# First modulation summed by VectorE, silu when the vectors are there, latent keys ahead of the values

## The reference

```python
cond = silu(c)                                    # 1024 values
for i in range(4):
    mod = cond @ ada_w[i] + ada_b[i]              # 1024 x 6144
    sh_a, sc_a, g_a, sh_f, sc_f, g_f = split(mod, 6)
    h = rms_norm(x, norm_g[i, 0]) * (1 + sc_a) + sh_a
    y = mixer(h)                                  # MLA in layers 0 and 3
    ...

def mla_mixer(h):                                 # 8 heads
    q_lat, kv_lat, k_pe = split(h @ w_in, [256, 384])
    q = rms_norm(q_lat, q_norm) @ w_q_up          # 128 + 64 (rope) a head
    kv = rms_norm(kv_lat, kv_norm) @ w_kv_up      # 128 keys, 128 values a head
    # q, k get rope parts; causal softmax in query blocks of 128; then @ w_out
```

## Time and profile before

| | us |
|---|---|
| median of three runs | 4621.73 |
| lowest and highest | 4619.29, 4622.21 |
| the profiled execution | 4615.57 |
| its span, first to last instruction | 4613.8 |
| TensorE busy | 4290.5 (93%) |
| mean granted TensorE clock | 0.947 |

### The profile page before, as it was taken

One profiled execution on the slowest core, in us unless ns is written; L12 is line 12 of the kernel. 1 busy time (PEld: TensorE's weight loads), 2 busy tenths in 40 slices (PEclk: granted clock), 3 DMA queues, 4 the chain that ended last, 5 costly groups with the idle time before them and its releaser, 6 DMA issues.

```text
span 4613.8 us, 66591 instructions
## 1 busy us (share of the span) xinstructions
PE 4290.5 (93%) x24442; PEld 2275.2 (49%) x24442; DVE 2171.8 (47%) x4420; ACT 2498.2 (54%) x3432; POOL 1951.3 (42%) x1077
## 2 busy tenths in 40 slices
PE   7989989889989988998989989998899899999999
PEld 5544444444444434444544443445455565556555
DVE  4654220644152423424521021426469887586684
ACT  4557444667444535744567444356456555655544
POOL 1134333444333324443034333220135456858767
PEclk9989989989989998998989989798899899999999
DMA  4346222046222223622022222220123456958768
GB/s 160 144 166 237 96 80 83 16 171 223 96 84 79 73 69 143 254 96 82 24 73 100 100 89 86 71 71 1 37 98 132 164 196 216 336 194 290 261 216 300
DMA packets 160504, 623.63 MB, mean 135 GB/s; under 512 B 17824, under 2 KB 17952, under 8 KB 156816
## 3 DMA queue, kind: packets, MB, share of 16 engines
q1 hardware_dynamic: 123120, 483.65, 30.0%
q0 software_dynamic: 37152, 136.80, 8.0%
HBM read 618.29 MB, written 2.10 MB: 134 GB/s over the span
## 4 chain that ended last, share of the span: by engine, by line
PE 58%; issue 17%; POOL 12%; DVE 9%; DMA 2%; ACT 2%; POOLq 0%; DVEq 0%; ACTq 0%
PE ps L779 15%; PE ps L780 15%; PE ps L781 15%; POOL halves L592 8%; POOL rows L660 3%; PE ps L830 2%; DMA rows<-v_rows,h 1%; DVE rows L2593 1%; PE ps L1373 1%; PE ps L786 1%; PE ps L788 1%; PE ps L787 1%; PE ps L717 1%; POOL x L642 1%; DVE rows L2592 1%
## 5 line engine op out<-in xcount | busy, mean ns | idle before, releaser
L592 POOL TENSOR_TENSOR halves<-ring,halves 128x1024 f16<-128x1024 f32 x718 | 1583.1, 2206 | 2438.9 <-ACT halves L1480 2205.0
L779 PE MATMUL ps<-h,halves 128*128 128x512 f16 (+1 forms) x2912 | 1061.3, 364 | 42.7 <-DVE h L2162 21.1
L780 PE MATMUL ps<-h,halves 128*128 128x512 f16 (+1 forms) x2912 | 1060.6, 364 | 0.0
L781 PE MATMUL ps<-h,halves 128*128 128x512 f16 (+1 forms) x2912 | 1059.4, 364 | 0.0
L1477 ACT ACTIVATE ring<-ring 128x1024 f32<-128x1024 f32 x718 | 754.7, 1051 | 479.7 <-DMA ring<-wstream 406.5
L779 PE MATMUL ps<-rows,halves 128*128 128x512 f16 (+2 forms) x2544 | 914.5, 359 | 83.7 <-POOL halves L592 40.1
L780 PE MATMUL ps<-rows,halves 128*128 128x512 f16 (+2 forms) x2544 | 913.0, 359 | 0.0
L781 PE MATMUL ps<-rows,halves 128*128 128x512 f16 (+2 forms) x2544 | 912.1, 359 | 0.0
L1480 ACT ACTIVATE halves<-ring 128x1024 f16<-128x1024 f32 x718 | 758.8, 1057 | 22.8
L779 PEld LDWEIGHTS ps<-h,halves 128*128 128x128 f16 x2912 | 287.0, 99 | 354.2 <-issue 60.8
L781 PEld LDWEIGHTS ps<-h,halves 128*128 128x128 f16 x2912 | 287.3, 99 | 296.6 <-issue 13.1
(11 more groups left out here) (290 smaller groups left out, 5053.5 us busy)
## 6 DMA issues: line engine op xcount, KB each, us to landing
ring<-wstream SPq DMA_DIRECT2D x718, 512.0 KB, 3.3
rows<-ada SPq DMA_DIRECT2D x96, 768.0 KB, 5.1
rows<-ada_first SPq DMA_DIRECT2D x24, 1024.0 KB, 5.5
x<-x_in POOLq DMA_DIRECT2D x1, 2048.0 KB, 13.3
rows<-u_rows,h POOLq DMA_INDIRECT x128, 5.8
rows<-v_rows,h POOLq DMA_INDIRECT x128, 6.2
out<-x SPq DMA_DIRECT2D x8, 256.0 KB, 2.7
rows<-phase_nsa SPq DMA_DIRECT2D x1, 1600.0 KB, 6.6
```

Of the source, the lines that this page charges most:

```text
L592: nc.gpsimd.tensor_tensor(halves[:, j % RING, 1, :], ring[:, j % RING, :], halves[:, j % RING, 0, :], ALU.subtract).then_inc(s_wlow, 1)
L779: nc.tensor.matmul(out_, high, act16[:, 0, :], start=first, stop=False)
L780: nc.tensor.matmul(out_, high, act16[:, 1, :], start=False, stop=False)
L781: return nc.tensor.matmul(out_, low, act16[:, 0, :], start=False, stop=last)
```

## The change

- `EARLY_SUMS` is 8: VectorE sums all eight chunks of the first modulation, three of them, then its two pair sums of squares, three more, the inverse roots, then the last two. TensorE only sums the finished buffer over the partitions, with `ada_sums(0, 16, 8)`, after the token norms are spread.
- The vectors have a semaphore of their own, `s_vec`. ScalarE and VectorE start silu and the chunk sums when the vectors are there, and wait for `x` and the matrices (`s_const` at 32) only before the squares and before the modulation.
- The slots for keys and values change places. TensorE makes the key tiles first, through the four banks as before; then the value tiles, through banks 4 to 7, with a wait that the inverses have been copied from bank 5 (`s_latcopied`) and with their own count of reads. ScalarE reads value tiles only after all key tiles have been read. VectorE starts the key products when the query and rotation tiles have been read.
- `row_blocks` on TensorE gets `late`: scores start when all but the last `late` = 8 reads (the value tiles) are done, and the wait for all of them stands before the first transpose.

```diff
-EARLY_SUMS = 4
+EARLY_SUMS = C
 ADA_PIECES = 6
...
         s_const = sem("consts_loaded")
+        s_vec = sem("vectors_loaded")
         s_phase = sem("phase_loaded")
...
         s_keys = sem("key_tiles")
+        s_latcopied = sem("latent_inverses_copied")
         s_negmax = sem("row_max_normed")
...
-            pool.dma_start(vec[:, :], vecs).then_inc(s_const, 16)
+            pool.dma_start(vec[:, :], vecs).then_inc(s_vec, 16)
             pool.dma_start(x[:, :, :], x_in).then_inc(s_const, 16)
...
-            def row_blocks(rows, places):
-
-                pe.wait_ge(s_evac, seen["tile"])
+            def row_blocks(rows, places, late):
+                pe.wait_ge(s_evac, seen["tile"] - late)
                 base_seg, base_pt, base_group, base_row = seen["seg"], seen["pt"], seen["group"], seen["row"]
...
+                        if i == lag:
+                            pe.wait_ge(s_evac, seen["tile"])
                         pe.wait_ge(s_normed, base_row + i - lag + 1)
...
                 input_means(h, IN_NORM[0])
-                seen["ada"] += EARLY_SUMS
-                pe.wait_ge(s_adas, EARLY_SUMS)
-                b = bank()
-                for j in range(2 * C):
-                    nc.tensor.matmul(b[:, j:j + 1], ada_sum[:, j * P:j * P + P], ones[:, 0:1], start=(j == 0), stop=False,
-                                     skip_group_check=True)
                 token_norms(IN_NORM[1])
-                pe.wait_ge(s_cond, 1)
-                for k in range(EARLY_SUMS, C):
-                    pe.wait_ge(s_adae[k], 16)
-                    for j in range(2 * C):
-                        mm = nc.tensor.matmul(b[:, j:j + 1], ada_early[:, k, j * P:j * P + P], cond[:, k:k + 1],
-                                              start=False, stop=(k == C - 1), skip_group_check=True)
-                mm.then_inc(s_tile, 1)
+                ada_sums(0, 2 * C, EARLY_SUMS)
...
                 w = slot()
-                for tb in range(TB):
-                    for half in range(2):
-                        b = bank()
-                        mm = split_tokens(b, w, slice(half * T, half * T + T), latent16[:, 2],
-                                          slice(tb * P, tb * P + P), True, True)
-                        mm.then_inc(s_used if tb == TB - 1 and half else s_tile, 1)
-                w = slot()
                 for m in range(8):
...
+                w = slot()
+                pe.wait_ge(s_latcopied, layer // 3 + 1)
+                for tb in range(TB):
+                    for half in range(2):
+                        t = seen["tile"]
+                        if 2 * tb + half >= 4:
+                            pe.wait_ge(s_evac, t - 3)
+                        seen["tile"] += 1
+                        mm = split_tokens(ps[:, 4 + (2 * tb + half) % 4, :], w, slice(half * T, half * T + T),
+                                          latent16[:, 2], slice(tb * P, tb * P + P), True, True)
+                        mm.then_inc(s_used if tb == TB - 1 and half else s_tile, 1)
                 wait(s_rot, "rot", 5)
-                row_blocks(mla_rows(), mla_places)
+                row_blocks(mla_rows(), mla_places, 8)
...
                       "nsa": lambda l: nsa()}
-            pe.wait_ge(s_const, 48)
+            pe.wait_ge(s_vec, 16)
+            pe.wait_ge(s_const, 32)
             pe.wait_ge(s_ones, 4)
...
                             copy(y[:, 4 + i, :])
-                act.wait_ge(s_latinv, seen["lat"])
-                for m in range(8):
-                    b = tile(int(m == 7))
-                    nc.scalar.activation(arena[:, 20 + m, :], b, ACT.Identity, scale=kv_inv[:, m // 2:m // 2 + 1])\
-                        .then_inc(s_evac, 1)
...
                 use(1)
+                act.wait_ge(s_latinv, seen["lat"])
+                act.wait_ge(s_evac, seen["tile"])
+                for m in range(8):
+                    if m < 7:
+                        seen["tl"] += 1
+                        act.wait_ge(s_tile, seen["tl"])
+                    else:
+                        seen["used"] += 1
+                        act.wait_ge(s_used, seen["used"])
+                    seen["tile"] += 1
+                    nc.scalar.activation(arena[:, 20 + m, :], ps[:, 4 + m % 4, :], ACT.Identity,
+                                         scale=kv_inv[:, m // 2:m // 2 + 1]).then_inc(s_evac, 1)
+                feed(seen["used"] + AHEAD)
                 row_blocks(mla_rows(), mla_places)
...
-            act.wait_ge(s_const, 48)
             act.wait_ge(s_ones, 3)
+            act.wait_ge(s_vec, 16)
             nc.scalar.activation(cond[:, :], v("c", 0, C), ACT.Silu).then_inc(s_cond, 1)
             nc.scalar.preload_act_table_set("sqrt_and_others")
+            act.wait_ge(s_const, 32)
             for k in range(C):
...
                 dve.wait_ge(s_latspread, seen["mla"] + 1)
-                link(nc.vector.tensor_copy(rinv, ps[:, KV_NORM[1], :]))
+                nc.vector.tensor_copy(rinv, ps[:, KV_NORM[1], :]).then_inc(s_latcopied, 1)
+                dve.wait_ge(s_latcopied, seen["mla"] + 1)
                 for m in range(8):
...
                     else:
-                        dve.wait_ge(s_used, seen["used"] + 4 + 3 + 1 + 1)
+                        dve.wait_ge(s_used, seen["used"] + 4 + 3 + 1)
                     if m == 0:
-                        tiles(6 + 8)
+                        tiles(6)
                     mul(arena[:, 12 + m, :], ps[:, (seen["tile"] + m) % LIN_BANKS, :], rinv)\
                         .then_inc(s_evac, 1)
-                tiles(8)
+                seen["tile"] += 16
                 row_blocks(mla_rows(), mla_places,
...
-            dve.wait_ge(s_const, 48)
+            dve.wait_ge(s_vec, 16)
             if stages[0][1] < LAYERS:
                 dve.wait_ge(s_cond, 1)
-                ada_third(0, range(EARLY_SUMS // 2))
+                ada_third(0, range(3))
                 square_pairs(h)
-                ada_third(0, range(EARLY_SUMS // 2, EARLY_SUMS))
+                ada_third(0, range(3, 6))
                 inverse_roots()
+                ada_third(0, range(6, C))
+                dve.wait_ge(s_const, 32)
                 tiles(1)
...
                 feature_slots(np.concatenate([q[:, :, MLA_NOPE:].reshape(256, -1), q[:, :, :MLA_NOPE].reshape(256, -1)], 1)),
-                kv[:, :, 1].reshape(1, P, SLOT), kv[:, :, 0].reshape(1, P, SLOT),
+                kv[:, :, 0].reshape(1, P, SLOT), kv[:, :, 1].reshape(1, P, SLOT),
                 feature_slots(a["mla_w_out"][j])]
...
```

## The result

| | us |
|---|---|
| before, median of 4 runs | 4621.81 |
| after, median of 4 runs | 4574.24 (4568.31 to 4575.36) |
| ratio after to before, with its 95% interval | 0.9896 (0.9878 to 0.9913) |
| profiled execution and span, after | 4568.31, 4566.3 |
| mean granted TensorE clock | 0.954 (before 0.947) |

What follows compares the result with a forecast made beforehand. TensorE, busy for 93% of the span, was taken to bound the kernel. Minus 20.1 us (start) and minus 6.3 us (latent stages) make minus 26.4, from a 4621.73 us median to 4595 us, range 4586 to 4603.

Steps and rivals of the forecast that it cites:

- Part 1: First modulation at the start: 128 single-column matmul records go, column matmuls end at 45.4 us, minus 20.1 us.
- The turns with GpSimd: Start: two GpSimd subtractions and VectorE's last two chunk sums exclude each other, ending the sums at 38.3, not 34.8 us.
- rival A: Start: VectorE isn't held up by GpSimd, so the first modulation gives 23.6 us; 4591.8 us, chance 17%.
- Part 2: Latent stage of both MLA layers: keys ahead of values start the scores 3.15 us earlier, twice, minus 6.3 us.
- ScalarE's lateness: Latent stage: ScalarE gains only 1.5 us, but the first row is ready 1.0 us before its transpose at 136.1.
- Rival C: Latent stage: the new order gives nothing, the wait only moves to the first transposes; 4601.6 us, chance 13%.
- The sum: Whole kernel: minus 20.1 minus 6.3 = minus 26.4 us, so 4595 us; forecast's chance 50%.
- rival B: Layer 3's first score rows: without idles the half-clock fall may stay away, 7.9 us more; 4587.4 us, chance 17%.
- So the whole kernel moves by this amount: Everything behind the first projection: nothing has a clock of its own, so all shifts by the start's 20.1 us.
- Rival D: Start: the eighth chunk becomes the pacemaker and the kernel is slower if it lands from 62.3 us on; chance 1%.

Runs made afterwards that it cites:

- e7: Changed kernel, but GpSimd makes its first two weight subtractions only after VectorE's eight chunk sums; ratio 0.9888 to the kernel before.
- e14: Kernel before with only the first latent-stage idle filled by unread matmuls, the 1.51 us ahead of the scores kept; 4629.27 us, ratio 0.9999.
- second part alone: Kernel before with only keys ahead of values and values in other banks, the start as before; 4605.16 us, ratio 0.9942.
- e1: Kernel before with only the first modulation's part of the change, the latent stage as before; 4611.85 against 4631.45 us, ratio 0.9963.
- e10: Kernel before, not edited, run once more with a second profile; 4633.17 us in one run.
- e13: Kernel before with only the idle ahead of the scores filled by unread matmuls, the first idle kept; 4615.24 against 4629.49 us, ratio 0.9973.
- e9: Changed kernel, not edited, run again with a second profile; 4583.63 against 4627.96 us for the kernel before, ratio 0.9905.
- e3: Changed kernel with four of the sixteen column matmuls on the finished modulation sum made twice; ratio 0.9905 to the kernel before.
- e12: Changed kernel with GpSimd's subtractions held behind the sums and unread matmuls in TensorE's waits at the start; 4579.73 us, ratio 0.9900 to the kernel before.

## Why the prediction was wrong

- **Part 1, the start: right.** 45.4 was forecast for the end of the column matmuls, 45.46 came; VectorE's last sum at 38.3, came at 38.42; the projection at 48.7, came at 48.88. The turns with GpSimd, the one real choice in this part, were right (e7), and rival A is out. Two small readings were off and cost nothing: the squares started at 18.00, not 17.3, and silu ran at 10.03, not 8, since its table load waited for the vectors, until 8.74; in the kernel before that load was over before any input had landed (below). Alone the part measured 17 us (11 to 24).
- **Part 2, the order: right.** 10.7 us from keys to scores, both idles gone (with an unchanged start, 59.81 us from the first projection to the first score in e14, with the old order and its first idle filled, and 56.68 with the second part alone), ScalarE's lateness hidden with 0.9 us to spare, 1.0 forecast. Rival C is out: the first row was ready at 111.30, its transpose started at 112.21.
- **The sum: wrong, in the term that it left out.** The prediction said of the half clock in layer 3, "layer 0 had the same idles and no fall, so it isn't the idles alone", gave rival B 17%, and put its price at 7.9 us in one layer. The runs showed it to be the idle ahead of the scores, in both layers as a rule: with that idle, layer 3 fell in four profiles of four (before, e1, e10, e14) and layer 0 in three of four; without it, or with 1.23 us, in none of the twelve others. In the table below, a fall cost some 8 us in layer 3, and 7.9 (e1) or 12.6 us (e10, e14) in layer 0. What both are worth in the medians is 12.5 us (e13; 8 to 17), taken by a line that moves nothing. 26.4 + 12.5 = 38.9, where 47.6 and 44 us were measured (interval of the second 37 to 51).
- **The step behind that.** One absent event in layer 0 is one sample, and I used it as evidence against a mechanism that layer 3 showed at its full price. "The median shown is 6.2 above it, with the same work" passed over a hint that single executions differ. It was no more than a hint: the changed kernel's two profiled executions are 5.9 and 6.7 us under their medians as well, with no fall behind the latent stage, so the distance doesn't say which stretch is missing.
- **A second step that failed: "So the whole kernel moves by this amount".** It doesn't move as one piece. These are the parts of the span, in us, with the row blocks taken up to the next matmul on converted weights (207.48 in the kernel before):

| profile | to first projection | to layer 0's first score | its row blocks | to layer 3's first score | its row blocks | to the end |
|---|---|---|---|---|---|---|
| before | 68.81 | 63.72 | 74.95 | 2017.66 | 82.92 | 2305.70 |
| before again (e10) | 69.17 | 62.40 | 87.57 | 2017.31 | 82.92 | 2312.00 |
| second idle kept (e14) | 69.54 | 59.81 | 87.58 | 2017.34 | 82.91 | 2312.97 |
| first idle kept (e13) | 69.60 | 59.72 | 74.98 | 2019.87 | 75.04 | 2311.41 |
| first part alone (e1) | 48.75 | 59.82 | 82.85 | 2022.77 | 82.92 | 2311.57 |
| changed | 48.88 | 56.72 | 74.87 | 2010.36 | 74.94 | 2300.57 |
| changed again (e9) | 48.80 | 56.79 | 74.87 | 2010.43 | 74.93 | 2309.06 |
| delayed by the smaller amount (e3) | 50.22 | 58.99 | 74.88 | 2016.10 | 74.94 | 2308.65 |

From the first profile of the kernel before to that of the changed kernel, the columns differ by 19.9, 7.0, 0.1, 7.3, 8.0 and 5.1 us. The forecast's terms are 20.1, 3.15 in the second and 3.15 in the fourth. The second column has 3.4 us more from a half-clock stretch ahead of layer 0's latent stage, with TensorE busy in all of it, which the changed kernel's two profiles lack:

```profile
94.20:101.00 6.80, 6.80 (x18) 0.50 0.12 47
```

The fourth has some 4 us more from the work between the layers, where the same number of matmul records kept TensorE busy for 1873.0 us in place of 1879.9; in e3 they took 1881.1. So in these two profiles layer 3's fall is 8.0 of the missing 21 us. Most of the rest is the 3.4 and 4 us, which were largely back when the start moved by 1.3 us (e3: 58.99 and 2016.10), and 5.1 us behind layer 3.

- **Open.** 5 to 9 us between 38.9 and the measured medians. The table shows places where a single profile gains that much, and shows them for the changed kernel twice, alike to 0.1 us up to layer 3. But its other runs took 5.6 to 7.1 us longer, in the first set at a mean granted clock of 0.951 against the profile's 0.954, and no profile shows where. The last column differs by 8.5 us between two profiles of one kernel, so nothing is read from it. Why 1.51 us bring the fall and 1.23 don't isn't settled either; one profile and 4 runs stand behind the 1.23.
- Rival D didn't occur: the sum ended 6.7 us behind the landing forecast from the profile before (31.7), and the time lies in the turns with GpSimd.

## What to carry to other kernels

An idle of TensorE is priced by itself plus what its clock does behind it: look at the granted clock right after every idle, and price what runs there at the level that the rows show. Where the idle can't go, a few matmuls that nobody reads can fill it: seven in each of the two layers were worth 12.5 us here, and their row blocks took 0.1 us longer than in the changed kernel. A fall that is absent once, in one profile, may be there in most executions; a second profile is worth more than a finer sum from the first.

## What the runs showed of the hardware that I had not expected

- Behind 1.51 us of idle ahead of the scores the granted clock fell to half for 17 to 27 us, through rows on which TensorE was busy nearly without a gap (10.66 us of 10.70 in e14, granted 0.56). The level has to be read from the clock column; the busy share doesn't show it.
- Single-column float32 matmuls: 32 records took 6.99 us at the start and 3.89 us in e12, behind eleven unread matmuls of 512 columns, at a granted clock of 1.00. The clock has no record for the first 52.8 us of the changed kernel's profile; that 6.99 us is the half level is read from the 512-column matmul that follows, 0.58 us for 0.38.
- When ScalarE's table load for silu runs depends on the waits written ahead of silu. In the kernel before, `s_const` stands first and `s_ones` last, and the load ran at 3.49 us, while the activation itself waited for the matrices until 17.28. In the changed kernel the wait for the vectors stands last, and the load started with their landing, at 8.74; with silu late, the matrices' stands last, and it started at 17.93. In all three it began when the wait written last was over. Before and silu late:

```profile
3.49 1.28 ACT L1999 ACT_TABLE_LOAD   x1 [3.49 <-POOL eps_weighted L600]
...
17.93 1.28 ACT L2007 ACT_TABLE_LOAD   x1 [17.93 <-DMA lasting<-mats]
```
